# First attention of a two-block network: gate chunks as seven half products

## Chip, cores and metric

One Trainium2 chip, one core of it, one launch. The metric is device time in microseconds; lower is better. TensorE (PE) multiplies into PSUM, VectorE (DVE) and ScalarE (ACT) work on SBUF and PSUM, GpSimd (POOL) on SBUF, and SyncE (SP) issues the weight transfers.

## What is computed

The network has a first block and two layers of a second block, all in float32 on 256 tokens (512 with context) and 1024 features. The change touches the gates of the first block's mixer. Cut to what matters:

```
h = rms_norm(x, attn_pre_norm)                       # 256 x 1024
proj = h @ w_in                                      # a_qkv | b_q | b_kv | c_qkv | gates
o_a, o_b, o_c = dilated_attention(..), sliding_window_gqa(..), stick_breaking_attention(..)
g = sigmoid(gates.reshape(b, s, 3, 1024) + b_gate)   # gates: 3072 columns
merged = g[0] * (o_a @ w_br_a) + g[1] * (o_b @ w_br_b) + g[2] * (o_c @ w_br_c)
return merged @ w_out
```

The gates need h alone, so their product with 3072 columns of `w_in` can stand anywhere before `merged`.

## The kernel before

Weights come as a stream of chunks of 1024 x 256 numbers (1 MB) into a ring of four slots (`ring`). SP requests chunk c when PE has finished chunk c - 4 (`chunk_done`). Activations stand features by tokens in `H`; the 256 tokens of the first block use its columns 0 to 255.

The first attention runs in 32 **units** (`units1`): one head and one half of 128 queries each. Units 0 to 7 are branch a (three groups of keys at once), 8 to 23 branch b, 24 to 31 branch c (stick breaking, no softmax). Even units see 128 keys a group, odd ones 256. In each turn u of the loop PE does, in a written order: `scores1(u)`, the first half of a filling chunk, `turn1(u-1)` (transposes of the probabilities), the second half, `values1(u-1)`. DVE does `probs1(u-1)` (normalising, or for branch c a chain with a scan), `rows1(u)` (bias and row maximum), `turned1(u-1)` (copy of the transposed probabilities out of PSUM), then its part of the filling chunk. ACT does the exponentials, its part of the filling chunk and the copy of the values. Each engine keeps this order, so a long step on DVE holds all that stands behind it.

The filling chunks are `gates` in units 1, 4 and 6 of every eight (`GATE_AT`; twelve chunks of 256 columns) and the modulation `ada0` (24 chunks, M = 32, short). A gate chunk is two half chunks of eight matmuls of 256 tokens into PSUM bank pair 0; DVE adds the bias to one half and ACT to the other in the same unit, as soon as the whole chunk is done (`beside`, `gate_out`).

Other places of the kernel already form a chunk by **seven half products** instead of eight (`pe_fast`): four of 128 x 128 x 128 matmuls each, three with the weights as they are and four with sums of weights that POOL makes (`pool_sums`, four additions of 128 x 512 a chunk into `SUMS`, two buffers), and with differences of the activations that DVE makes once (`dve_turn`). ACT and DVE then put the four blocks together from the products (`act_fast`, `dve_fast`). The gated feed-forward of the first block (`upv`) does so with 128 tokens a product. In the first attention POOL has nothing to do.

Of the kernel before, what the change touches and what calls it, by code (L numbers as in the profile page):

```python
# [9 lines left out]
P = 128  # L10
D = 1024
KT = D // P
T1 = 256
# [3 lines left out]
SLOTS = 4  # L17
# [111 lines left out]

FAST = {"upv": 1, "down": 4, "q0": 1, "k0": 1, "v0": 1, "k1": 1, "v1": 1, "ssd_o0": 2, "out20": 1, "mlp1a0": 1, "mlp2a0": 2, "mlp1b0": 1, "mlp2b0": 2, "mlp11": 1, "mlp21": 4}  # L130
FIRST_SET = {"upv": 1, "down": 0, "q0": 1, "k0": 0, "v0": 0, "k1": 0, "v1": 0, "ssd_o0": 0, "out20": 1, "mlp1a0": 1, "mlp2a0": 0, "mlp1b0": 0, "mlp2b0": 0, "mlp11": 1, "mlp21": 0}
WIDTH = {"upv": P, "down": P, "mlp11": P, "mlp21": P}
ONE_SIDE = ("upv",)

# [34 lines left out]
def fast_plan():  # L169

    groups, chunks, used, n = {}, {}, [0, 0], 0
    for name, j in ORDER:
        if name not in FAST:
            continue
        chunks.setdefault(name, []).append(n)
        n += 1
        if j % FAST[name] == 0:
            g = groups.setdefault(name, [])  # L180
            side = (FIRST_SET[name] + len(g) * (name not in ONE_SIDE)) % 2
            g.append((sum(used), side, used[side]))
            used[side] += 1
    return groups, chunks
# [28 lines left out]
def program(nc, xT, stream, params, rows, consts, rel_bias, rev_hot, w_dt, scratch, cs_rows, x_kept, mrg_kept, out):  # L213
    ctx = ExitStack()
    with ctx:
# [255 lines left out]

        fast_free = [sem("fast_free0"), sem("fast_free1")]
        swapped = [sem("q_swapped"), sem("k_swapped")]
# [233 lines left out]
        def act_fast(act, name, keep, then_=None, beside_=None, only=None):  # L707


            share, width = FAST[name], WIDTH.get(name, T1)  # L710
            for i, (f, side, before) in enumerate(FAST_GROUPS[name]):
                if only is not None and i != only:
                    continue
                if name in ("v0", "v1"):
                    act.wait_ge(sem("v_group"), (0 if name == "v0" else 4) + i + 1)
                else:
                    act.wait_ge(chunk_done, CHUNKS[name][share * i + share - 1] + 1)
                nc.scalar.activation(keep[side], fast_bank(side, 2)[:, 0:width], ACT.Copy).then_inc(sem("fast_kept"), 1)  # L718
# [180 lines left out]
        HM1 = area(B1_GATE, 4, 4, P)  # L899
        HID1_T = area(B1_GATE + 2048, 4, 16, P)  # L900

        U_L = [area(B1_TMP + 768 * i, 768) for i in range(2)]
# [174 lines left out]
        def _(pe):  # L1077
# [62 lines left out]
            def ada_second(name, j):  # L1140
# [12 lines left out]
                mm.then_inc(sem("ada_turned"), 1)  # L1153

            def beside(items, T, t):

                if t == 0:
                    held.finish(ada_second)
                for name, j in items:
                    modulation = name.startswith("ada")  # L1160
                    if modulation and t == 0:
# [86 lines left out]
            pe.wait_ge(sem("u_out_read"), len(units1))  # L1248
            pe.wait_ge(sem("u_read_a"), len(units1) - N_AB)

            def sums_behind(tag):
# [458 lines left out]
        def _(act):  # L1710
# [38 lines left out]

            def gate_out(bank, j, it):  # L1750
                return copy(one(GATE, 2 * j + 1, 2, it), bank[:, 0:T1], ACT.Identity,
                            bias=par[:, span(PARAMS["b_gate"][0] + 2 * j + 1, 2, it)])

            bar()
# [15 lines left out]
            def beside(items, op):  # L1770
                for name, j in items:
                    if name.startswith("ada"):
                        if j % ADA_RUN == ADA_RUN - 1:
                            held.pending = (name, j)
                        continue
                    pair, before = GROUPS[name][j]
# [43 lines left out]
            pair, before = GROUPS["gates"][-1]  # L1820
            act.wait_ge(evacuated[pair], 2 * before + 2)
            for j in range(4):
# [464 lines left out]
        def _(v):  # L2287
# [64 lines left out]

            def gate_out(bank, j, it):
# [116 lines left out]
            for u in range(len(units1) + 1):  # L2470
# [4 lines left out]
                if u >= 1:  # L2475
                    turned1(u - 1)
                if u < len(units1):
                    beside(attention_fill(-1)[u], gate_out)
            for j in range(4):
# [587 lines left out]
        def _(pool):  # L3067
# [19 lines left out]
            pool.wait_ge(sem("bias_in"), 16)  # L3087
            bar()

            for j in range(4):  # L3090
# [267 lines left out]
```

## Time and profile before

| | |
|---|---|
| median of 3 runs | 2996.71 us (2996.35 to 3005.4) |
| profiled execution | 3000.34 us, its span 2998.5 us |
| mean granted PE clock | 0.994 |
| PE busy | 2923.9 us, 98% of the span |
| DVE, ACT, POOL busy | 48%, 27%, 34% |
| first attention | units begin at 128.71 us, branch products at 312.24 us |

Times in the rows count from the span's start. PE is busy nearly always, but the number counts matmuls that overlap; whether a stage is bound by PE or by the chain of waits between the engines is read from idle time in brackets in the timeline. Float32 matmuls have two records each, so "x16" is eight matmuls.

### The profile page before, as it was taken

What the parts mean: (1) busy time and instruction counts of PE and PEld (TensorE: products, weight loads), DVE (VectorE), ACT (ScalarE), POOL (GpSimd) and SP (SyncE); (2) the same over time, 40 slices, a digit from 0 to 9 for tenths busy, and PEclk for the clock granted to TensorE, in tenths of its full rate; (3) what the DMA queues carried; (4) which work ended last, traced back from release to release, by engine and by line L of the source; (5) the groups of instructions that cost most, each with busy time, mean ns of one, the idle gap of its engine ahead of it and who ended that gap; (6) DMA issues with size and microseconds to landing.
All of it is one profiled execution on the core that took longest, in us unless ns stands there. A gap on an engine that the chain in (4) does not pass through costs nothing.

```text
span 2998.5 us, 40516 instructions
## 1 busy us (share of the span) xinstructions
PE 2923.9 (98%) x16088; PEld 2388.8 (80%) x16088; DVE 1453.4 (48%) x2765; ACT 814.4 (27%) x1778; POOL 1020.8 (34%) x876
## 2 busy tenths in 40 slices
PE   8999999999999999999999999999998999999999
PEld 7776789998865548888878888888886666678998
DVE  1243268722255647777753442342237555541651
ACT  1022132201022316666610220110114355540210
POOL 0000134484310115565654244443330112110786
PEclk9999999999999999999999999999999999999999
DMA  7455434442355232222232122222330332334443
GB/s 260 142 201 219 155 127 163 161 169 99 99 185 206 87 128 100 112 105 107 90 135 84 71 85 84 87 97 85 112 113 29 128 106 99 113 107 153 155 169 113
DMA packets 68977, 377.63 MB, mean 126 GB/s; under 512 B 6378, under 2 KB 24874, under 8 KB 26304
## 3 DMA queue, kind: packets, MB, share of 16 engines
q1 hardware_dynamic: 49120, 334.60, 30.8%
q10 hardware_dynamic: 18704, 36.90, 3.7%
q0 software_dynamic: 976, 3.63, 0.3%
q8 instruction: 127, 2.08, 0.3%
q14 instruction: 50, 0.41, 0.0%
HBM read 366.50 MB, written 4.42 MB: 124 GB/s over the span
## 4 chain that ended last, share of the span: by engine, by line
PE 61%; DVE 7%; ACT 2%; PEld 1%; issue 1%; POOL 0%; PEldq 0%; POOLq 0%; ACTq 0%; DVEq 0%
PE PB L501 12%; PE PB L629 9%; PE PA L501 7%; PE PB L1480 6%; PE PS L501 6%; PE PB L381 5%; PE PB L1187 2%; PE PB L1453 2%; PE PB L425 2%; PE PA L1540 1%; PE PA L1576 1%; PE PA L1559 1%; DVE work L2871 1%; ACT work L1951 1%; PE PB L1494 1%; DVE small L2670 1%
## 5 line engine op out<-in xcount | busy, mean ns | idle before, releaser
L536 POOL TENSOR_TENSOR sums<-ring 128x512 f32<-128x512 f32 x115 | 151.6, 1318 | 603.8 <-PE PA L501 247.1
L501 PE MATMUL PB<-work,sums 128*128 128x128 f32 (+1 forms) x1360 | 230.5, 327 | 0.0
L1480 PE MATMUL PB<-H,ring 128*128 128x512 f32 (+1 forms) x576 | 228.2, 545 | 0.0
L501 PEld LDWEIGHTS PB<-work,sums 128*128 128x128 f32 x1360 | 207.0, 191 | 17.6
L501 PE MATMUL PA<-work,sums 128*128 128x128 f32 (+1 forms) x1280 | 208.9, 318 | 0.0
L734 DVE TENSOR_TENSOR work<-PA,work 128x128 f32<-128x128 f32 (+1 forms) x53 | 18.9, 357 | 379.6 <-ACT work L718 379.6
L501 PEld LDWEIGHTS PA<-work,sums 128*128 128x128 f32 x1280 | 187.4, 191 | 13.6
L3170 POOL TENSOR_TENSOR work<-work 128x256 f32<-128x256 f32 x96 | 59.8, 644 | 386.3 <-ACT work L2039 327.1
L1480 PEld LDWEIGHTS PB<-H,ring 128*128 128x128 f32 x576 | 108.4, 190 | 95.2 <-issue 90.9
L1187 PE MATMUL PB<-H,ring 128*128 128x256 f32 (+1 forms) x640 | 175.5, 429 | 0.4 <-DVE rstd L2387 0.2
L734 DVE TENSOR_TENSOR work<-PB,work 128x256 f32<-128x256 f32 (+1 forms) x34 | 13.0, 381 | 320.8 <-ACT work L718 320.8
L1187 PEld LDWEIGHTS PB<-H,ring 128*128 128x128 f32 x640 | 120.4, 193 | 46.5 <-issue 33.0
L541 POOL TENSOR_TENSOR sums<-ring,sums 128x512 f32<-128x512 f32 x115 | 151.9, 1321 | 9.0
L381 PE MATMUL PB<-work,ring 128*128 128x256 f32 (+1 forms) x544 | 153.0, 442 | 1.5 <-DVE work L2775 0.7
L539 POOL TENSOR_TENSOR sums<-sums,ring 128x512 f32<-128x512 f32 x115 | 149.7, 1302 | 0.0
L537 POOL TENSOR_TENSOR sums<-ring 128x512 f32<-128x512 f32 x115 | 148.7, 1293 | 0.0
L718 ACT ACTIVATE work<-PS 128x128 f32<-128x128 f32 (+1 forms) x53 | 17.5, 330 | 478.1 <-PE PA L501 431.1
L501 PE MATMUL PB<-work,ring 128*128 128x128 f32 (+1 forms) x840 | 143.5, 325 | 0.0
L629 PE MATMUL PB<-work 128*128 128x256 f32 x624 | 143.2, 382 | 0.0
L381 PEld LDWEIGHTS PB<-work,ring 128*128 128x128 f32 x544 | 103.0, 190 | 49.9 <-issue 39.6
L501 PEld LDWEIGHTS PB<-work,ring 128*128 128x128 f32 x840 | 127.0, 191 | 10.4
L501 PE MATMUL PS<-work,ring 128*128 128x128 f32 (+1 forms) x760 | 133.7, 319 | 0.0
(439 smaller groups left out, 5980.1 us busy)
## 6 DMA issues: line engine op xcount, KB each, us to landing
ring<-stream SPq DMA_DIRECT2D x314, 1024.0 KB, 4.8
sums<-cs_rows ACTq DMA_DIRECT2D x16, 1024.0 KB, 4.6
sums<-cs_rows ACTq DMA_DIRECT2D x16, 512.0 KB, 3.8
work<-work ACTq DMA_DIRECT2D x16, 256.0 KB, 4.5
work<-scratch POOLq DMA_DIRECT2D x1, 2560.0 KB, 13.6
mrg_kept<-work ACTq DMA_DIRECT2D x1, 2048.0 KB, 10.4
work<-mrg_kept ACTq DMA_DIRECT2D x1, 2048.0 KB, 10.6
X<-xT SPq DMA_DIRECT2D x2, 512.0 KB, 5.7
```

The source lines that it names most:

```text
L381: mm = pe.matmul(PB[:, pair, t, 0:T], ring[:, c % SLOTS, k, t * P:(t + 1) * P], rhs(k), start=(k == 0), stop=(k == KT - 1))
L425: mm = pe.matmul(PB[:, pair, t, 0:T], ring[:, c % SLOTS, k, t * P:(t + 1) * P], rhs(KT * part + k), start=(part == 0 and k == 0), stop=(pa ...
L501: mm = pe.matmul(fast_bank(side, bank)[:, col:col + width], weight(k), right(4 * part + k), start=first and opens and k == 0, stop=last an ...
L536: nc.gpsimd.tensor_tensor(su[:, 0], a21, a22, ALU.add).then_inc(sem("w_summed"), 1)
L537: nc.gpsimd.tensor_tensor(su[:, 2], a11, a21, ALU.subtract).then_inc(sem("w_summed"), 1)
L539: nc.gpsimd.tensor_tensor(su[:, 1], su[:, 0], a11, ALU.subtract).then_inc(sem("w_summed"), 1)
L541: nc.gpsimd.tensor_tensor(su[:, 3], a12, su[:, 1], ALU.subtract).then_inc(sem("w_summed"), 1)
L629: mm = pe.matmul(fast_bank(0, bank)[:, col:col + T1], weight(k), right(k), start=opens and k == 0, stop=k == 3, skip_group_check=True)
L1187: mm = pe.matmul(PB[:, pair, t, 0:T], ring[:, c % SLOTS, k, t * P:(t + 1) * P], H[:, k, 0:T], start=(k == 0), stop=(k == KT - 1))
L1453: mm = pe.matmul(PB[:, pair, t, 0:T], ring[:, c % SLOTS, k, t * P:(t + 1) * P], H[:, k, 0:T], start=(k == 0), stop=(k == KT - 1))
L1480: mm = pe.matmul(PB[:, pair, t, 0:Tc], ring[:, c % SLOTS, k, t * P:(t + 1) * P], H[:, k, 0:Tc], start=(k == 0), stop=(k == KT - 1))
L3170: gp.tensor_tensor(XD[d].rearrange("p (a b) -> p a b", a=4), XG[:, t, :].rearrange("p (a b) -> p a b", a=4), WD[:, t, heads].unsqueeze(2). ...
```

## The change

All twelve gate chunks go over to seven half products of 128 tokens. `dve_turn` makes the differences of h once, early, into the free half of `H`. POOL makes the weight sums of each chunk (`pool_sums(pool, "gates")`) from the end of the barrier before the units. PE does four products where the first half chunk stood and three where the second stood (`gate_products`). The seven results lie in bank pair 0's first half and ACT copies one of them (`act_fast`); DVE puts the blocks together in `gate_out`, seven operations, **one turn later**, behind `turned1(u-1)`; the next gate chunk and the end of the stage wait for that (`fast_free[2]`).

```diff
+            def gate_products(j, t):
+                c, n = CHUNKS["gates"][j], FAST_CHUNKS["gates"][j]
+                w, su = ring[:, c % SLOTS], SUMS[:, n % 2]
+                def product(bank, high, opens, weight, right):
+                    for k in range(4):
+                        mm = pe.matmul(gate_part(bank, high), weight(k), right(k), start=opens and k == 0, stop=k == 3,
+                                       skip_group_check=True)
+                    return mm
+                if t == 0:
+                    take_chunk(pe, c, 0, 0)
+                    if j:
+                        pe.wait_ge(fast_free[2], j)
+                    product(2, 0, True, lambda k: w[:, 2 * k, 0:P], lambda k: H[:, 2 * k, 0:P])
+                    product(0, 0, True, lambda k: w[:, 2 * k + 1, 0:P], lambda k: H[:, 2 * k + 1, 0:P])
+                    product(3, 0, False, lambda k: w[:, 2 * k + 1, P:2 * P], lambda k: h1_turned(3, k))
+                    pe.wait_ge(sem("w_summed"), 4 * n + 1)
+                    product(2, 1, False, lambda k: su[:, 0, k, :], lambda k: h1_turned(0, k))
+                    return
+                pe.wait_ge(sem("w_summed"), 4 * n + 2)
+                product(1, 1, False, lambda k: su[:, 2, k, :], lambda k: h1_turned(2, k))
+                pe.wait_ge(sem("w_summed"), 4 * n + 3)
+                product(0, 1, False, lambda k: su[:, 1, k, :], lambda k: h1_turned(1, k))
+                pe.wait_ge(sem("w_summed"), 4 * n + 4)
+                product(1, 0, False, lambda k: su[:, 3, k, :], lambda k: H[:, 2 * k + 1, P:T1]).then_inc(chunk_done, 1)
...
+                    if name == "gates":
+                        act_fast(act, name, H1_KEEP[0:1] * 3, only=j)
+                        continue
...
+            dve_turn(v, H[:, :, 0:T1], [H[:, 4 * (n % 2):4 * (n % 2) + 4, T1 + P * (n // 2):T1 + P * (n // 2) + P]
+                                        for n in range(4)], 4,
+                     lambda: v.wait_ge(sem("n1_h"), 2 * KT), sem("h1_turned"), P)
...
-            def gate_out(bank, j, it):
-                return vec.tensor_scalar(one(GATE, 2 * j, 2, it), bank[:, 0:T1],
-                                         par[:, span(PARAMS["b_gate"][0] + 2 * j, 2, it)], None, ALU.add)
+            def gate_out(j):
+                f, side, before = FAST_GROUPS["gates"][j]
+                keep, (u2, u4, u3) = H1_KEEP[0], H1_U
+                bias = [p_("b_gate", 2 * j + t) for t in range(2)]
+                v.wait_ge(sem("fast_kept"), f + 1)
+                vec.tensor_tensor(u2, gate_part(0, 1), keep, ALU.add).then_inc(sem("dve_step"), 1)
+                u2_done = next_step(dve_steps)
+                vec.scalar_tensor_tensor(GATE[:, 2 * j, 0:P], gate_part(0, 0), bias[0], keep, ALU.add, ALU.add)
...
+                vec.tensor_tensor(u4, gate_part(2, 1), u2, ALU.add).then_inc(sem("dve_step"), 1)
+                vec.tensor_tensor(u3, gate_part(1, 1), u2, ALU.add).then_inc(sem("dve_step"), 1)
+                for t in range(2):
+                    vec.scalar_tensor_tensor(GATE[:, 2 * j + t, P:T1], gate_part(1, t), bias[t], u4, ALU.add, ALU.add)
+                vec.scalar_tensor_tensor(GATE[:, 2 * j + 1, 0:P], u3, bias[1], gate_part(3, 0), ALU.add, ALU.subtract)\
+                    .then_inc(fast_free[2], 1)
...
                 if u >= 1:
                     turned1(u - 1)
+                if u and u - 1 in GATE_AT:
+                    gate_out(GATE_AT.index(u - 1))
                 if u < len(units1):
-                    beside(attention_fill(-1)[u], gate_out)
+                    beside([x for x in attention_fill(-1)[u] if x[0] != "gates"], None)
...
             bar()
+            pool_sums(pool, "gates")
```

The order of PE's instructions shows it at units 17 and 18, a gate unit of branch b and the one behind it. L1205 are scores, L1187 the gate chunk, L1218 transposes, L1227 values, L1179 an `ada0` chunk. Before:

```order
L1205 MATMUL PB<-work 128x256
L1187 MATMUL PB<-H,ring 128x256 x8
L1218 MATMUL PA<-con,work 128x128
L1187 MATMUL PB<-H,ring 128x256 x8
L1227 MATMUL PA<-work 64x128
L1205 MATMUL PS<-work 128x128
L1218 MATMUL PA<-con,work 128x128 x2
L1179 MATMUL PA<-ring,cact 32x256 x8
L1227 MATMUL PA<-work 64x128 x2
```

Now (L1250 scores, L1176 products, L1263 transposes, L1272 values, L1224 `ada0`):

```order
L1250 MATMUL PB<-work 128x256
L1176 MATMUL PB<-H,ring 128x128 x12
L1176 MATMUL PB<-H,sums 128x128 x4
L1263 MATMUL PA<-con,work 128x128
L1176 MATMUL PB<-H,sums 128x128 x12
L1272 MATMUL PA<-work 64x128
L1250 MATMUL PS<-work 128x128
L1263 MATMUL PA<-con,work 128x128 x2
L1224 MATMUL PA<-ring,cact 32x256 x8
L1272 MATMUL PA<-work 64x128 x2
```

Nothing else moved on PE: sixteen matmuls of 256 tokens became twenty-eight of 128 around the same transposes.

DVE at the same place. L2354 is the old `gate_out`, L2447 to L2450 are `probs1`, L2414 to L2420 `rows1`, L2466 is `turned1`. Before, from the end of unit 17's chunk:

```order
L2354 TENSOR_SCALAR work<-PB,par 128x256
L2447 TENSOR_TENSOR small<-small 128x1
L2449 RECIPROCAL small<-small 128x1
L2450 TENSOR_SCALAR work<-work,small 128x256
L2414 TENSOR_TENSOR work<-PS,work 128x128
L2419 TENSOR_REDUCE small<-work 128x1
L2420 TENSOR_TENSOR small<-small 128x1
L2466 COPY work<-PA 128x256
L2447 TENSOR_TENSOR small<-small 128x1
```

Now, from `probs1(17)` on (L2511 to L2514 `probs1`, L2478 to L2484 `rows1`, L2530 `turned1`, L2406 to L2418 the new `gate_out`):

```order
L2511 TENSOR_TENSOR small<-small 128x1
L2513 RECIPROCAL small<-small 128x1
L2514 TENSOR_SCALAR work<-work,small 128x256
L2478 TENSOR_TENSOR work<-PS,work 128x128
L2483 TENSOR_REDUCE small<-work 128x1
L2484 TENSOR_TENSOR small<-small 128x1
L2530 COPY work<-PA 128x256
L2406 TENSOR_TENSOR work<-PB,work 128x128
L2408 SCALAR_TENSOR_TENSOR work<-PB,par,work 128x128
L2410 TENSOR_TENSOR work<-PB,work 128x128
L2412 TENSOR_TENSOR work<-PB,work 128x128
L2416 SCALAR_TENSOR_TENSOR work<-PB,par,work 128x128 x2
```

One operation in front of `probs1(17)` went, and seven (with a last L2418) stand between `turned1(17)` and `probs1(18)`.

## Rows read from the trace of the kernel before

**Rows 1.** Waits of PE in 128:312 (us in total, times, longest)

```profile
PE PA L1218 <- DVE work L2441: 5.0, 3, 2.5
```

**Rows 2.** Timeline of PE, units 17 and 18 (start us, us, instructions, [idle before])

```profile
233.25 0.44 PE L1218 MATMUL PA<-con,work 128*128 128x128 f32 x2 [0.46 <-DVE work L2450]
...
235.82 0.33 PE L1218 MATMUL PA<-con,work 128*128 128x128 f32 x1
```

**Rows 3.** Timeline of PE in the feed-forward: plain chunk, seven half products, plain chunk

```profile
409.16 7.07 PE L1303 MATMUL PB<-H,ring 128*128 128x256 f32 x32
416.07 1.05 PE L501 MATMUL PS<-H,ring 128*128 128x128 f32 x8
...
422.32 7.07 PE L1303 MATMUL PB<-H,ring 128*128 128x256 f32 x32
```

**Rows 4.** Timeline of DVE: first evacuation of a projection chunk

```profile
28.66 0.42 DVE L2342 TENSOR_SCALAR work<-PB 128x256 f32<-128x256 f32 x1 [1.91 <-PE PB L381]
```

**Rows 5.** Timeline of DVE in the feed-forward (convolution steps, block assembly)

```profile
404.16 1.78 DVE L2547 SCALAR_TENSOR_TENSOR work<-PB,par,work 128x255 f32<-128x255 f32 x4 [3.34 <-ACT work L1857]
409.67 0.29 DVE L734 TENSOR_TENSOR work<-PA,work 128x128 f32<-128x128 f32 x1 [3.73 <-ACT work L718]
409.88 0.28 DVE L736 TENSOR_TENSOR work<-PA,work 128x128 f32<-128x128 f32 x1
```

**Rows 6.** Timeline of DVE, units 17 and 18

```profile
233.10 0.28 DVE L2414 TENSOR_TENSOR work<-PS,work 128x128 f32<-128x128 f32 x1
...
233.82 0.42 DVE L2466 COPY work<-PA 128x256 f32<-128x256 f32 x1
234.71 0.16 DVE L2447 TENSOR_TENSOR small<-small 128x1 f32<-128x1 f32 x1 [0.46 <-ACT work L1801]
...
235.10 0.29 DVE L2450 TENSOR_SCALAR work<-work,small 128x128 f32<-128x128 f32 x1
```

**Rows 7.** Timeline of DVE: `probs1(15)`, `turned1(20)`, `probs1(23)`

```profile
221.32 0.16 DVE L2447 TENSOR_TENSOR small<-small 128x1 f32<-128x1 f32 x1 [0.27 <-ACT work L1801]
...
247.68 0.29 DVE L2466 COPY work<-PA 128x128 f32<-128x128 f32 x1
...
260.43 0.16 DVE L2447 TENSOR_TENSOR small<-small 128x1 f32<-128x1 f32 x1 [0.71 <-ACT work L1801]
```

**Rows 8.** Timeline of PE: end of gate 14, start of gate 22, `turn1(25)`

```profile
217.01 1.07 PE L1179 MATMUL PA<-ring,cact 128*32 128x256 f32 x16
...
248.80 3.72 PE L1187 MATMUL PB<-H,ring 128*128 128x256 f32 x16
...
273.65 0.44 PE L1218 MATMUL PA<-con,work 128*128 128x128 f32 x2 [1.78 <-DVE work L2441]
```

**Rows 9.** Timeline of DVE in the feed-forward: `dve_turn` without and with POOL at work

```profile
399.79 0.29 DVE L758 TENSOR_TENSOR work<-work 128x128 f32<-128x128 f32 x1
...
414.86 1.24 DVE L758 TENSOR_TENSOR work<-work 128x128 f32<-128x128 f32 x1
```

**Rows 10.** Timeline of POOL at that time

```profile
414.21 1.73 POOL L536 TENSOR_TENSOR sums<-ring 128x512 f32<-128x512 f32 x1 [8.05 <-DMA ring<-stream]
415.91 1.31 POOL L537 TENSOR_TENSOR sums<-ring 128x512 f32<-128x512 f32 x1
```

**Rows 11.** One line's instructions, L2600: duration ns min/median/max

```profile
L2600 DVE TENSOR_SCALAR work<-work,par x8: 346/982/1356, 621.3 to 696.6; 128x256 f32<-128x256 f32 x8
```

**Rows 12.** One line's instructions, L734: duration ns min/median/max

```profile
L734 DVE TENSOR_TENSOR work<-PB,work x34: 290/424/425, 619.8 to 2961.6; 128x256 f32<-128x256 f32 x23, 128x128 f32<-128x128 f32 x11
```

**Rows 13.** Landing of weight chunks (SP's issues, 128:312)

```profile
DMA to landing us min/median/max: 4.6/4.8/7.8
```

**Rows 14.** Timeline of DVE: first and last operation of `probs1(25)`, branch c

```profile
271.53 0.42 DVE L2435 TENSOR_TENSOR work<-work 128x256 f32<-128x256 f32 x1
...
273.17 0.42 DVE L2441 TENSOR_TENSOR work<-work 128x256 f32<-128x256 f32 x1
```

**Rows 15.** Busy time by stretch: us, PE, PEld, DVE, ACT, POOL, PEclk, DMA, GB/s

```profile
275.20:285.40 10.20, 10.20 (x38) 6.28 (x38) 2.75 (x9) 1.65 (x6) 0.00 (x0) 0.50 0.58 212
```

More of the change, by code:

```diff
@@ L127, in chunk_order @@
     return order
[L130 to L133, printed above, removed]
+FAST = {"gates": 1, "upv": 1, "down": 4, "q0": 1, "k0": 1, "v0": 1, "k1": 1, "v1": 1, "ssd_o0": 2, "out20": 1, "mlp1a0": 1, "mlp2a0": 2, "mlp1b0": 1, "mlp2b0": 2, "mlp11": 1, "mlp21": 4}
+FIRST_SET = {"gates": 2, "upv": 1, "down": 0, "q0": 1, "k0": 0, "v0": 0, "k1": 0, "v1": 0, "ssd_o0": 0, "out20": 1, "mlp1a0": 1, "mlp2a0": 0, "mlp1b0": 0, "mlp2b0": 0, "mlp11": 1, "mlp21": 0}
+WIDTH = {"gates": P, "upv": P, "down": P, "mlp11": P, "mlp21": P}
+ONE_SIDE = ("upv", "gates")
 SCAN_FAST = ("ssd0", "z0", "gs0")
@@ L169, in fast_plan @@
 def fast_plan():
-    groups, chunks, used, n = {}, {}, [0, 0], 0
+    groups, chunks, used, n = {}, {}, [0, 0, 0], 0
     for name, j in ORDER:
@@ L180, in fast_plan @@
             g = groups.setdefault(name, [])
-            side = (FIRST_SET[name] + len(g) * (name not in ONE_SIDE)) % 2
+            side = FIRST_SET[name] if name in ONE_SIDE else (FIRST_SET[name] + len(g)) % 2
             g.append((sum(used), side, used[side]))
@@ L470, in fast_bank, with gate_part @@
                 else (PA[0], PA[1], PS[:, 0], PS[:, 1])[i]
-        fast_free = [sem("fast_free0"), sem("fast_free1")]
+        def gate_part(bank, high):
+            at = 2 * P * (bank % 2) + P * high
+            return PB[:, 0, bank // 2, at:at + P]
+        fast_free = [sem("fast_free0"), sem("fast_free1"), sem("fast_free2")]
         swapped = [sem("q_swapped"), sem("k_swapped")]
@@ L717, in act_fast @@
                     act.wait_ge(chunk_done, CHUNKS[name][share * i + share - 1] + 1)
-                nc.scalar.activation(keep[side], fast_bank(side, 2)[:, 0:width], ACT.Copy).then_inc(sem("fast_kept"), 1)
+                kept = gate_part(2, 0) if name == "gates" else fast_bank(side, 2)[:, 0:width]
+                nc.scalar.activation(keep[side], kept, ACT.Copy).then_inc(sem("fast_kept"), 1)
                 if beside_:
@@ L900, in program, with h1_turned @@
         HID1_T = area(B1_GATE + 2048, 4, 16, P)
+        H1_KEEP = [area(25608 + P * i, P) for i in range(2)]
+        H1_U = [area(25864 + P * i, P) for i in range(3)]
+        def h1_turned(n, q):
+            return H[:, 4 * (n % 2) + q, T1 + P * (n // 2):T1 + P * (n // 2) + P]
         U_L = [area(B1_TMP + 768 * i, 768) for i in range(2)]
@@ L1249, in _ @@
             pe.wait_ge(sem("u_read_a"), len(units1) - N_AB)
+            pe.wait_ge(fast_free[2], len(GATE_AT))
             def sums_behind(tag):
@@ L1748, in _ @@
             evac(act, 1, "c_v", lambda bank, j, it: copy(V1[:, 1, 896:1152], bank[:, 0:CHUNK], ACT.Copy))
-            def gate_out(bank, j, it):
-                return copy(one(GATE, 2 * j + 1, 2, it), bank[:, 0:T1], ACT.Identity,
-                            bias=par[:, span(PARAMS["b_gate"][0] + 2 * j + 1, 2, it)])
             bar()
@@ L1774, in beside @@
                             held.pending = (name, j)
+                        continue
+                    if name == "gates":
+                        act_fast(act, name, H1_KEEP[0:1] * 3, only=j)
                         continue
@@ L1814, in _ @@
                     softmax1(u)
-                    beside(attention_fill(-1)[u], gate_out)
+                    beside(attention_fill(-1)[u], None)
                 if u >= 1:
@@ L1818, in _ @@
             held.finish(ada_second)
-            pair, before = GROUPS["gates"][-1]
-            act.wait_ge(evacuated[pair], 2 * before + 2)
+            act.wait_ge(fast_free[2], len(GATE_AT))
             for j in range(4):
@@ L2476, in _ @@
                     turned1(u - 1)
+                if u and u - 1 in GATE_AT:
+                    gate_out(GATE_AT.index(u - 1))
                 if u < len(units1):
-                    beside(attention_fill(-1)[u], gate_out)
+                    beside([x for x in attention_fill(-1)[u] if x[0] != "gates"], None)
             for j in range(4):
```

7 lines of the change are left out of this document (6 added, 1 removed).

## Prediction

> **What bounds the kernel now.** I read the page first (PE busy 98%, so time is won only where PE's own work shrinks and PE really is what is waited for), then PE's timeline and its waits from 128 to 312 us, then DVE's, ACT's and SP's timelines of the same units, and last the feed-forward stage, which already runs the form that the gates are to get. In the first attention PE mostly has work, but not everywhere: it sits idle ahead of transposes until DVE has made the probabilities. The reader is to see three such waits behind branch c's last step, 5.0 us in all, 2.5 the longest [rows 1]; 1.78 us of it stand at unit 25 [rows 8]. They follow gate units: the old `gate_out` waits for the whole chunk and holds `probs1` of the same unit, so the next transposes are late. At unit 18 the same thing costs 0.46 us [rows 2]. So this stage hangs between PE and DVE, and a change that takes work from PE and gives work to DVE is to be costed on both.
>
> **The change part by part.**
>
> *PE's work.* In the feed-forward a plain chunk of 32 records starts at 409.16 and the seven half products behind it at 416.07: 6.91 us. These last until 422.32: 6.25 us [rows 3]. So a gate chunk gets 0.66 us shorter, not an eighth of its multiplications' 6.91 (0.86). The split around the transposes stays as it is. Twelve chunks: **-7.9 us**.
>
> *Waits that go.* `gate_out` no longer stands in front of `probs1` of its own unit. The waits at units 9 and 17, 0.46 us each ([rows 2], of which unit 9 is a repeat), 25 with 1.78 [rows 8] and 28 with the remaining 5.0 - 2.5 - 1.78 = 0.7 [rows 1] lose their cause: **-3.4 us**. The one of 2.5 is at unit 31, behind the last `ada0` chunk, and stays.
>
> *Waits that come: DVE.* The new `gate_out` has three two-tensor additions, which the block assembly of the feed-forward issues 0.21 us apart, and four operations with a bias. A convolution step of this kind on 255 columns takes 1.78 / 4 = 0.44 us [rows 5]; 127 columns fewer at the 0.13 us by which 128 columns more lengthen such operations (0.29 to 0.42 in [rows 6]) leave 0.31. Sum 0.6 + 1.2 = 1.8 us, against 0.4 of the old one. It stands behind `turned1(u-1)`, and queued behind it are `probs1(u)`, for which PE's next transposes wait, and `rows1` of the next unit.
> - Units 2, 5: branch a's fill is long enough, nothing. Units 13 and 21: `probs1` is hidden behind the next gate chunk's first half, but that chunk needs the bank that `gate_out` is still reading. `turned1(20)` starts at 247.68 and gate 22 at 248.80 [rows 7, 8]: 247.68 + 0.2 + 1.8 = 249.7, so +0.9. The same at 14, and about 0.4 at 30: +2.2.
> - Units 10, 18, 26, directly behind a gate of the pattern's first place. From the end of its scores, unit 18 needs on DVE its rows (233.10 to 233.82, 0.72), the copy (0.35), now 1.8, and its probabilities (234.71 to 235.39, 0.68): 3.6 us [rows 6]. PE, which then starts `turn1(17)` at once, is at `turn1(18)` after 235.82 - 233.25 = 2.57 us [rows 2]. Wait about 1.1; 1.4 in branch c, whose chain is longer: +3.6.
> - Units 7, 15, 23, behind a gate unit that has an `ada0` chunk too. DVE's slack ahead of the probabilities is only 0.27 us at 15 and 0.71 at 23 (7 is like 23) [rows 7]; 1.8 less that is 1.5 + 1.1 + 1.1: +3.7.
>
> Sum: **+9.5 us**.
>
> *Waits that come: POOL.* Up to now POOL is idle in this stage. A subtraction on 128 columns with both inputs in SBUF takes 0.29 us while POOL rests and 1.24 while POOL adds weights: it starts at 414.86 and ends at 416.10, just behind the end of POOL's operation at 415.94 [rows 9, 10]. A scalar product from SBUF goes from 0.35 to as much as 1.36 us [rows 11]. Operations with an input in PSUM don't suffer: all of the assembly's additions stay within 0.43 us, whatever POOL does in those stages [rows 12], so `gate_out` itself is safe. In the attention the blocked kinds are the tiny sum and the scaling in `probs1` (branch b), and all four operations of branch c's chain. The Trainium skill ("SBUF — State Buffer", section "SBUF: two separate sides") says that a VectorE operation in a two-port mode or with two SBUF inputs and a GpSimd operation that reads SBUF exclude each other for a whole instruction. The rows agree; no row here shows the scan of branch c beside POOL, which by that rule is held as well, and without which the sum would be about 1 us less.
>
> When does POOL run? A gate's weights are requested when the chunk four ahead is done and land 4.8 us later [rows 13]; then four additions of 1.3 us [rows 10]. For gate 17 that chunk is gate 14, done at 217.01 [rows 8]: POOL runs from 221.8 to 227, right on `probs1(15)`, which [rows 7] put at 221.3 and the new `gate_out` at 222.8. Two held operations there: +1.3. Gate 25 hangs on gate 22 in the same way and hits `probs1(23)`: +1.5. Gates 9 and 17 lose about 0.9 together at units 7 and 17. For gate 28 the transfers queue, and POOL meets `probs1(25)`: four held operations of 1.3 us in place of the 2.06 us from 271.53 to 273.59 [rows 14] would keep the wait there at up to 2.9; it is a race with the landing, so I take half, 1.5. Sum **+5.2 us**, between 0 (all misses) and 7. The weights themselves come in time: gate 17's last sum is ready 4.8 + 5.2 = 10 us behind gate 14's end, and its last product, about 2 us ahead of the 233.25 of [rows 2], is due after 14.
>
> *The differences of h.* Four operations ahead of the first evacuation on DVE, each at most the 1.24 us of [rows 9] though POOL rests, together at most 5 us. DVE idles 1.91 us there [rows 4]; what runs over delays one evacuation whose bank PE wants a chunk later, 6.9 us on [rows 3]. Nothing; without that cover 3 us.
>
> *The clock.* The wait of 1.78 us at unit 25 was followed by a stretch of 10.2 us at a granted 0.50, the lower level, 1.2 GHz, on a PE that was busy throughout [rows 15]: 5.1 us. Now 15 and 23 get waits of about 3 us, and 25 keeps one. I count half of one more such stretch: **+2.5 us**, between 0 and 10.2 (two whole ones).
>
> Sum: -7.9 - 3.4 + 9.5 + 5.2 + 2.5 = **+5.9 us**. Against the profiled execution's 3000.34 us (span 2998.5 and 1.84 around it) that is 3006.2; that execution is 3.6 us above the median of the runs, as long as most of such a clock stretch. From the median of 2996.71: **3002.6 us**.
>
> **Rivals.** *DVE's work is hidden after all and POOL misses.* For it: DVE is busy less than half the time. Against it: rows 6 and 7 show the slack place by place. With half the new waits and no held operation: -7.9 - 3.4 + 4.8 = -6.5, 2990 us; with none of them -11.3, 2985.4. This is the case on the fast side; it wins by over 0.3% only if less than 2.3 us of new waits come.
>
> *The clock falls at each long wait.* Same sum with two whole stretches more: -7.9 - 3.4 + 9.5 + 5.2 + 10.2 = +13.6, 3010.3 us. It decides from the point where waits at 15 and 23 reach the 1.78 us that the one at unit 25 had. For it: the sum gives them 2.6 to 2.8. Against it: a stretch need not be 10 us long.
>
> *The change moves nothing,* because the stage is bound by DVE and ACT throughout: 2996.7. Against it: most gate halves follow each other on PE without idle time.
>
> **How the numbers follow.** 0.3% is 9.0 us, about what a measurement of this kernel can tell from no change. My sum, with part of one more clock stretch: 0.50, 2997 to 3006. Two whole stretches, or longer waits: 0.25, 3005 to 3012. Nothing moved: 0.08. Waits mostly hidden: 0.17, 2985 to 2995. Faster than 2987.7 is half of the last, 0.08. Slower than 3005.7 is the second and a little of the first, 0.28. Same: 0.64. The range leaves out a tenth on each side: from 2989, where half the DVE waits are hidden, to 3010, two stretches.
>
> **What the profile would show.** Gate halves of about 3.6 and 2.7 us. POOL in the stage with 12 x 5.2 = 62 us. No wait ahead of `turn1(9)` and `turn1(17)`; new ones of about 1 us ahead of `turn1` at 10 and 18, of 2.5 to 3.5 at 15 and 23, and 0.9 ahead of gates 14 and 22. `probs1(15)`'s two SBUF operations stretched to 1 us or more. A lower granted clock behind unit 15 or 23. The prediction is wrong if POOL's additions fall into gate halves in which DVE rests, or if `gate_out` takes much less than 1.8 us.

## The result, and the profile after

The changed kernel takes 3004.76 us (median of 20 runs, 2996.85 to 3015.39), the kernel before 2997.22 us in the same sessions (20 runs, 2995.49 to 3007.18). The ratio is 1.002, 95% interval 1.0011 to 1.0028: 3 to 8 us slower, under the 9 us that count as a change here (ratio and interval come from all runs, not from the two medians). Forecast were 3002.6 us and "same".

The page of the changed kernel, span and busy times of the engines:

```profile
span 2998.7 us, 41227 instructions
...
PE 2917.1 (97%) x16376; PEld 2394.4 (80%) x16376; DVE 1484.5 (50%) x2841; ACT 812.0 (27%) x1778; POOL 1081.0 (36%) x924
```

POOL has 60 us more than before (1020.8) and PE 7 us less. The gain on PE is there, and the time is not. PE's waits in 128:315, grouped (us in total, times, longest), say where it went; their counterpart is [rows 1]:

```profile
PE PA L1263 <- DVE work L2514: 6.8, 5, 2.1
PE PA L1263 <- DVE work L2505: 4.5, 3, 2.5
...
PE PB L1176 <- DVE work L2418: 2.1, 3, 0.9
PE PA L1164 <- DVE rstd L2432: 1.1, 1, 1.1
```

L2514 is `probs1`'s scaling, for which the transposes (L1263) wait; L2505 is the last operation of branch c's chain, for which they wait there; L2418 is `gate_out`'s last operation, for which the next gate chunk waits; L2432 is DVE's copy of a modulation run. The timeline of PE gives the places (start us, duration us, [idle before <- releaser]):

```profile
179.81 0.66 PE L1263 MATMUL PA<-con,work 128*128 128x128 f32 x4 [1.53 <-DVE work L2514]
...
196.19 0.33 PE L1263 MATMUL PA<-con,work 128*128 128x128 f32 x1 [0.80 <-DVE work L2514]
...
209.26 2.92 PE L1176 MATMUL PB<-H,ring 128*128 128x128 f32 x24 [0.87 <-DVE work L2418]
...
221.51 0.62 PE L1164 MATMUL PA<-con,rstd 128*128 128x24 f32 x4 [1.11 <-DVE rstd L2432]
...
223.67 0.69 PE L1263 MATMUL PA<-con,work 128*128 128x128 f32 x2 [1.54 <-DVE work L2514]
...
241.13 0.33 PE L1263 MATMUL PA<-con,work 128*128 128x128 f32 x1 [0.80 <-DVE work L2514]
...
267.47 0.44 PE L1263 MATMUL PA<-con,work 128*128 128x128 f32 x2 [2.12 <-DVE work L2514]
...
278.19 0.44 PE L1263 MATMUL PA<-con,work 128*128 128x128 f32 x2 [0.74 <-DVE work L2505]
...
282.08 0.33 PE L1263 MATMUL PA<-con,work 128*128 128x128 f32 x1 [1.25 <-DVE work L2505]
```

In order (gate 14 is the gate chunk of unit 14): `turn1(7)`, `turn1(10)`, gate 14, unit 15 (twice: ahead of a modulation run's turn and of `turn1(15)`), `turn1(18)`, `turn1(23)`, `turn1(25)`, `turn1(26)`; gate 22 waits 0.87 us like gate 14, gate 30 0.32 us. The waits of 0.46 us at units 9 and 17 [rows 2] are gone, and 25 has 0.74 in place of 1.78 us [rows 8]. DVE's timeline at units 17 and 18 shows both causes:

```profile
235.24 1.25 DVE L2514 TENSOR_SCALAR work<-work,small 128x256 f32<-128x256 f32 x1
...
238.44 0.43 DVE L2530 COPY work<-PA 128x256 f32<-128x256 f32 x1
238.78 0.28 DVE L2406 TENSOR_TENSOR work<-PB,work 128x128 f32<-128x128 f32 x1
...
240.40 0.15 DVE L2511 TENSOR_TENSOR small<-small 128x1 f32<-128x1 f32 x1
...
240.79 0.29 DVE L2514 TENSOR_SCALAR work<-work,small 128x128 f32<-128x128 f32 x1
```

From 238.78 to 240.40 DVE puts the gate's blocks together, and `probs1(18)` stands behind it; `turn1(18)` waits until 241.13. The first row is the other cause: a scaling that takes 0.35 us elsewhere takes 1.25 us, and it ends at 236.49, just behind this operation of POOL's, which ends at 236.33:

```profile
235.06 1.27 POOL L547 TENSOR_TENSOR sums<-ring,sums 128x512 f32<-128x512 f32 x1
```

The third is the clock. Busy time by stretch (us, PE, PEld, DVE, ACT, POOL, PEclk, DMA share, GB/s), behind units 7 and 15 and behind unit 31:

```profile
181.20:184.60 3.40, 3.40 (x24) 2.43 (x13) 1.15 (x5) 0.48 (x3) 0.00 (x0) 0.50 0.44 94
...
222.20:232.40 10.20, 8.73 (x43) 6.15 (x44) 4.75 (x13) 1.98 (x9) 4.95 (x5) 0.50 0.56 231
...
307.50:317.70 10.20, 8.58 (x24) 6.57 (x25) 0.81 (x2) 6.15 (x7) 0.00 (x0) 0.50 0.34 121
```

These stretches run at the lower level, 1.2 GHz. That behind unit 25 [rows 15] is gone, and two new ones follow the new waits at units 7 and 15. The wait of 2.12 us at unit 23 is followed by none.

### The profile page after: what moved, and what is told of

The parts are those of the page before. It is cut to its first block, busy times and chain, and to the rows that moved or that the text cites. A ratio compares the mean times of both kernels' runs of the same rounds, so it can differ in the third digit from the quotient of the medians.

```text
span 2998.7 us, 41227 instructions
## 1 busy us (share of the span) xinstructions
PE 2917.1 (97%) x16376; PEld 2394.4 (80%) x16376; DVE 1484.5 (50%) x2841; ACT 812.0 (27%) x1778; POOL 1081.0 (36%) x924
## 4 chain that ended last, share of the span: by engine, by line
PE 61%; DVE 7%; ACT 1%; PEld 1%; issue 1%; POOL 0%; PEldq 0%; POOLq 0%; ACTq 0%; DVEq 0%
PE PB L507 12%; PE PB L635 9%; PE PA L507 7%; PE PB L1526 6%; PE PS L507 6%; PE PB L381 5%; PE PB L1232 2%; PE PB L1499 2%; PE PB L425 2%; PE PA L1586 1%; PE PA L1622 1%; PE PA L1605 1%; DVE work L2937 1%; ACT work L1995 1%; PE PB L1540 1%; DVE small L2736 1%
## 5 line engine op out<-in xcount | busy, mean ns | idle before, releaser
L542 POOL TENSOR_TENSOR sums<-ring 128x512 f32<-128x512 f32 x127 | 166.5, 1311 | 797.1 <-DMA ring<-stream 256.9
L1526 PEld LDWEIGHTS PB<-H,ring 128*128 128x128 f32 x576 | 108.4, 190 | 95.2 <-issue 90.9
L547 POOL TENSOR_TENSOR sums<-ring,sums 128x512 f32<-128x512 f32 x127 | 167.3, 1317 | 10.0
L545 POOL TENSOR_TENSOR sums<-sums,ring 128x512 f32<-128x512 f32 x127 | 165.5, 1303 | 0.0
L543 POOL TENSOR_TENSOR sums<-ring 128x512 f32<-128x512 f32 x127 | 164.0, 1291 | 0.0
L725 ACT ACTIVATE work<-PB 128x128 f32<-128x128 f32 (+1 forms) x46 | 15.2, 330 | 450.6 <-PE PB L507 346.6
L507 PEld LDWEIGHTS PB<-work,ring 128*128 128x128 f32 x840 | 127.0, 191 | 10.4
L635 PEld LDWEIGHTS PB<-work 128*128 128x128 f32 x624 | 116.6, 190 | 17.6 <-issue 1.7
```

Source lines behind the costliest of these rows:

```text
L507: mm = pe.matmul(fast_bank(side, bank)[:, col:col + width], weight(k), right(4 * part + k), start=first and opens and k == 0, stop=last an ...
L542: nc.gpsimd.tensor_tensor(su[:, 0], a21, a22, ALU.add).then_inc(sem("w_summed"), 1)
L543: nc.gpsimd.tensor_tensor(su[:, 2], a11, a21, ALU.subtract).then_inc(sem("w_summed"), 1)
L545: nc.gpsimd.tensor_tensor(su[:, 1], su[:, 0], a11, ALU.subtract).then_inc(sem("w_summed"), 1)
L547: nc.gpsimd.tensor_tensor(su[:, 3], a12, su[:, 1], ALU.subtract).then_inc(sem("w_summed"), 1)
L635: mm = pe.matmul(fast_bank(0, bank)[:, col:col + T1], weight(k), right(k), start=opens and k == 0, stop=k == 3, skip_group_check=True)
```

## The experiments

"Stage" is the time from unit 0's scores to the first branch product in the profiled execution (before: 128.71 to 312.24 us). "Rest" is the span from there to its end, in which all fourteen kernels are alike. "Low" is the part of the stage at a granted clock of 0.50. Ratios are to the kernel before, with 95% intervals; a, b, c and so on are the places in the text below.

| kernel | median us | ratio | stage | low | rest |
|---|---|---|---|---|---|
| before | 2997.22 | 1 | 183.5 | 13.2 | 2686.3 |
| changed | 3004.76 | 1.002 (1.0011 to 1.0028) | 184.3 | 18.1 | 2686.8 |
| a. POOL without its sums | 2997.0 | 0.999 (0.9978 to 1.0002) | 176.9 | 7.0 | 2692.0 |
| b. one assembly operation | 2993.7 | 0.9977 (0.9961 to 0.9993) | 178.5 | 18.7 | 2687.0 |
| c. neither | 2984.51 | 0.9953 (0.9934 to 0.9971) | 167.7 | 4.1 | 2686.4 |
| d. assembly in its own unit | 3019.9 | 1.0065 (1.0043 to 1.0088) | 207.5 | 53.6 | 2686.8 |
| e. early assembly | 2998.69 | 0.9992 (0.9976 to 1.0009) | 174.4 | 6.7 | 2692.3 |
| f. half of it early | 2994.91 | 0.999 (0.998 to 0.9999) | 177.9 | 7.9 | 2686.6 |
| g. sums in pieces | 2995.51 | 0.9996 (0.9986 to 1.0005) | 180.3 | 10.4 | 2692.2 |
| h. e and g together | 2985.83 | 0.9957 (0.994 to 0.9974) | 169.0 | 4.9 | 2687.1 |
| i. h, PE kept busy | 2988.53 | 0.9959 (0.9943 to 0.9975) | 169.3 | 0 | 2682.8 |
| j. before, PE kept busy | 2998.0 | 0.9988 (0.9975 to 1.0) | 180.5 | 0 | 2693.2 |
| k. changed, PE kept busy | 3003.16 | 1.0008 (0.9995 to 1.002) | 190.1 | 10.2 | 2686.3 |
| l. h, last scaling first | 2979.75 | 0.9937 (0.9918 to 0.9956) | 165.9 | 0 | 2682.8 |

**a, b, c: the two costs, each away and both.** In a, `pool_sums` adds one column of 128 for the gates from the third chunk on:

```diff
+                m = 1 if name == "gates" and n >= 2 else P
+                su = su[:, :, :, 0:m]
```

> Left out: from the third gate chunk on POOL adds only one column of each weight sum instead of 128 (half the sums' values are stale), so POOL holds nothing of DVE's for long; PE and DVE do all their work. Theory (the saving on PE is eaten by three things: the 1.8 us block assembly on DVE, POOL holding DVE's scalings, and the clock): the scalings (L2514) take .3 us each time, the waits of PE in front of turn1(7), turn1(15) and turn1(23) fall by .4 to 1.5 us each, those at units 10, 18, 26 and 14, 22, 30 stay at .3 to 1.2 us; the stage (scores of unit 0 to the branch products, 184.3 us in the changed kernel's profile) is 4 to 6 us shorter, the time near 2999.5 us. Rival (the assembly alone eats it): the stage is no more than 1 us shorter. Rival (the clock alone): the waits stay, only the low-clock stretches differ.

The stage is 7.4 us shorter than the changed kernel's, and more than half of that is the clock's (11.1 us less at the lower level; the price stands under j). From the timeline of PE, units 7, 10, 15 and 23:

```profile
179.75 0.66 PE L1265 MATMUL PA<-con,work 128*128 128x128 f32 x4 [1.07 <-DVE work L2516]
...
194.68 0.33 PE L1265 MATMUL PA<-con,work 128*128 128x128 f32 x1 [0.80 <-DVE work L2516]
...
220.00 0.62 PE L1166 MATMUL PA<-con,rstd 128*128 128x24 f32 x4 [1.11 <-DVE rstd L2434]
...
259.80 0.44 PE L1265 MATMUL PA<-con,work 128*128 128x128 f32 x2 [1.44 <-DVE work L2516]
```

7 and 23 lose 0.5 and 0.7 us, 15 its second wait of 1.54; 25 has none. 10 and 18 keep their 0.80 to the digit, gates 14 and 22 have 0.86 for 0.87. So POOL's part and DVE's part are told apart by place. In b, `gate_out` keeps its last operation alone:

```diff
-                vec.tensor_tensor(u2, gate_part(0, 1), keep, ALU.add).then_inc(sem("dve_step"), 1)
...
+                vec.scalar_tensor_tensor(GATE[:, 2 * j + 1, 0:P], gate_part(1, 0), bias[1], keep, ALU.add, ALU.add)\
```

> Left out: six of the seven DVE operations that assemble a gate chunk (the rest of the gate tiles is a constant, written once by POOL at the first chunk); PE's half products and POOL's sums are all there. Theory: the new waits of PE behind units 10, 18, 26 (.80, .80, 1.25 us) and at gates 14, 22, 30 (.87, .87, .32) are gone, those at 7, 15, 23 fall by some .5 us each; the stage is 7 to 9 us shorter than the changed kernel's, the time near 2996. Rival (POOL's hold alone): those six waits shrink by no more than .3 us each, the time stays above 3002. Rival (the clock alone): the waits stay.

The waits at 10 and at gates 14, 22 and 30 are gone. Two of the six stayed, against the expectation, and both are longer than in the changed kernel (timeline of PE, `turn1(18)` and `turn1(26)`):

```profile
232.51 0.33 PE L1265 MATMUL PA<-con,work 128*128 128x128 f32 x1 [1.02 <-DVE work L2506]
...
274.01 0.35 PE L1265 MATMUL PA<-con,work 128*128 128x128 f32 x1 [1.81 <-DVE work L2497]
```

With DVE ahead by the missing work, `probs1(18)` and `probs1(26)` now fall on POOL's sums: the one's scaling takes 1.18 us, and of the other's four operations two take over a microsecond, the scan among them, which takes 0.42 us elsewhere (h, unit 30). From b's timeline of DVE:

```profile
271.06 1.36 DVE L2493 TENSOR_TENSOR_SCAN work<-work 128x128 f32<-128x128 f32 x1
...
272.46 1.17 DVE L2496 TENSOR_TENSOR work<-work,con 128x128 f32<-128x128 f32 x1
```

In c both costs are away.

> Left out: both, six of the seven assembly operations and all but a column of the weight sums, so that what stays is PE's part of the change. Theory: it shows the saving on PE by itself, 7.9 us of work and 3.4 us of waits off the stage of the kernel before (183.5 us), and no new wait above .3 us: a stage of 172 to 174 us, a time of 2985 to 2989. Rival (the saving was never there: weights or the chain of the softmax bound the stage): a stage above 180 us, waits on landings or on ACT in the place of those on DVE.

It is 15.8 us shorter in the stage than the kernel before, more than expected, and holds no new wait (timeline of PE: `turn1(23)` has 0.60 as before the change, and the branch products begin):

```profile
254.27 0.44 PE L1267 MATMUL PA<-con,work 128*128 128x128 f32 x2 [0.60 <-DVE work L2508]
...
296.30 5.49 PE L1320 MATMUL PB<-work,ring 128*128 128x256 f32 x12 [0.66 <-ACT work L1857]
```

The rival that the saving isn't there falls. From c, the assembly alone brings 9.2 us back (a), POOL alone 10.8 (b), both 16.6 (changed), all of the saving. The single ones make 20.0 together, since the clock falls differently in each: by the price of j (0.44 us for each us at the lower level), 1.3, 6.4 and 6.2 us of these are clock, estimated, and without it the assembly costs 7.9, POOL 4.4 and both 10.4.

**d: the assembly in its own unit,** behind `turned1(u-1)` and before `probs1(u)`.

```diff
-                if u and u - 1 in GATE_AT:
-                    gate_out(GATE_AT.index(u - 1))
                 if u < len(units1):
+                    if u in GATE_AT:
+                        gate_out(GATE_AT.index(u))
```

> Nothing left out: the assembly of a gate's blocks stands in its own unit again (behind that unit's rows, before the scaling of its probabilities), where the kernel before had its eviction. Theory: DVE now waits for the chunk's last product and holds the scaling of the same unit behind 1.8 us of assembly, so turn1 of the gates' own units waits 1 to 2 us at twelve places, and the waits behind units 10, 18, 26 and at 14, 22, 30 go: 5 to 15 us slower than the changed kernel, 3010 to 3020. Rival (the place of the assembly doesn't matter, only its work): within 2 us of the changed kernel.

15 us slower than the changed kernel. The stage is 23.2 us longer, about 15.6 of it by 35.5 us more of lower clock (estimated by the price of j), the rest by waits. These stand ahead of the transposes of the gates' own units, 0.5 to 5.4 us at ten of the twelve, 9 and 25 the longest, and those at 10, 18, 26 and at gates 14, 22, 30 are gone (timeline of PE):

```profile
195.05 0.69 PE L1263 MATMUL PA<-con,work 128*128 128x128 f32 x2 [2.50 <-DVE work L2514]
...
293.97 0.69 PE L1263 MATMUL PA<-con,work 128*128 128x128 f32 x2 [5.40 <-DVE work L2505]
```

So "one unit later" was needed; the place decides more than the work does.

**e, f: a better place.** The products of the first part are p20, p00, p30, p01, those of the second p21, p11, p10, each part in a bank of its own, so that `gate_first` can read the first while PE fills the second. The seven operations stay seven; in e they stand between `probs1(u)` and `rows1(u+1)`, in f the last four behind `turned1(u)`.

```diff
                 if u >= 1:
                     probs1(u - 1)
+                    if u - 1 in GATE_AT:
+                        gate_first(GATE_AT.index(u - 1))
+                        gate_out(GATE_AT.index(u - 1))
```

> Nothing left out. The four products of the gates' first part now fill one PSUM bank, the three of the second the other; the kept product is copied, and three of the seven assembly operations made, as soon as the first bank is done; all seven stand between the scaling of the gates' unit and the rows of the next one, where DVE idles about 1.75 us, in the place of behind the copy of the turned blocks. Theory: the assembly is hidden as far as POOL leaves DVE alone: the waits behind units 10, 18, 26 (.80, .80, 1.25 us) and at gates 14, 22, 30 fall to .3 us or less, those at 7, 15, 23 stay between those of the run with one operation and those of the changed kernel; a stage near 179 us (the run with one operation had 178.5), a time of 2992 to 2998. Rival (the work of the assembly counts, wherever it stands): the waits move to the rows and scalings of the next unit, the stage stays above 183 us.

> Nothing left out. As the run before in this call, but the four late assembly operations stand where the changed kernel has all seven, behind the copy of the turned blocks. Theory: 1.15 us are left there in the place of 1.73, so the waits behind units 10, 18 and 26 fall by about .6 us each, those at gates 14, 22, 30 too: a stage between the early version's and the changed kernel's, near 181 us. Rival (the place doesn't matter): the same as the early version within 1 us.

In e the waits at gates 14, 22, 30, at 15 and 25 went, that at 7 is 0.23 us as before the change, and the stage fell by 9.9 us. But 10, 18 and 26 kept theirs (0.91, 1.01, 2.12), against the expectation (timeline of PE, `turn1(18)`):

```profile
234.39 0.33 PE L1264 MATMUL PA<-con,work 128*128 128x128 f32 x1 [1.01 <-DVE work L2520]
```

Here the scaling takes 1.17 us beside POOL's last sum: b's miss again. f has a stage between e and the changed kernel, as expected, though of the three waits behind units 10, 18 and 26 only the first got shorter (0.28, 1.02 and 2.34 us). Neither median shows much; e's profile has a rest 5.5 us longer (last section).

**g, h: shorter operations on POOL.** Each sum of 512 columns as four of 128:

```diff
+                    for k in range(0, 4, step):
+                        ins = nc.gpsimd.tensor_tensor(to[:, k:k + step], x[:, k:k + step], y[:, k:k + step], op)
+                    ins.then_inc(sem("w_summed"), 1)
```

> Nothing left out. The changed kernel, with each of POOL's 512 column sums of the gates made in four instructions of 128 columns. Theory (POOL holds DVE's scaling until its running instruction ends): the scalings that took 1.06 to 1.25 us take .3 to .7 us, the waits in front of turn1(7), turn1(15) and turn1(23) fall by .4 to .8 us each; a stage 2 to 5 us shorter than 184.3, a time of 2998 to 3002. Rival (POOL slows DVE as long as any sum is under way): the scalings take as long as before and the stage stays within 1 us, or is longer by what the 12 more instructions of each chunk take.

> Nothing left out. Early assembly and the sums in four pieces together. Theory: the two costs fall together and what is left is near PE's own saving: a stage of 170 to 176 us (the run with neither cost had 167.7), a time of 2986 to 2992, some .2 to .35% under the kernel before. Rival (the costs don't add up, since either alone fills DVE's slack): no better than the early version alone by more than 1 us.

In g the scaling of unit 17, 1.25 us in the changed kernel, takes 0.71 us (timeline of DVE); POOL needs 1.7 us a sum for 1.27 (timeline of POOL, a sum in four pieces). The scaling ends at 232.83, while the pieces go on: DVE is held by the instruction that runs, not by POOL's being at work.

```profile
232.12 0.71 DVE L2521 TENSOR_SCALAR work<-work,small 128x256 f32<-128x256 f32 x1
```

```profile
231.82 1.74 POOL L546 TENSOR_TENSOR sums<-sums,ring 128x128 f32<-128x128 f32 x4
```

Alone it gains 4.0 us of stage, most of it clock (7.7 us less at the lower level, 3.4 by the price of j): `turn1(15)` waits 0.32 us for 1.54, but 7 only 0.14 us less than in the changed kernel, and 10 and 26 longer (1.09 and 1.79). With e's order nearly everything is back: h is within 1.3 us of c, and does all the work. `turn1(10)` and `turn1(18)` wait at most 0.11 us there, `turn1(26)` 0.32 us. DVE's timeline of h at unit 20 shows the early three from 239.53, the late four from 241.10, and the next unit's rows at 242.23:

```profile
239.53 0.28 DVE L2413 TENSOR_TENSOR work<-PB,work 128x128 f32<-128x128 f32 x1
...
241.10 0.29 DVE L2426 TENSOR_TENSOR work<-PB,work 128x128 f32<-128x128 f32 x1 [0.83 <-PE PB L1186]
...
242.23 0.42 DVE L2491 TENSOR_TENSOR work<-PB,work 128x256 f32<-128x256 f32 x1
```

**i, j, k: the clock.** PE multiplies for nobody ahead of long waits:

```diff
+            def keep_busy(n):
+                for i in range(n):
+                    pe.matmul(PS[:, 1, 0:P], ident, ident, start=True, stop=True)
```

> Nothing left out; 18 products of 128 columns whose result nobody reads are added ahead of turn1(31), where PE waits 2.52 us for the last scaling. Base: early assembly with the sums in four pieces. Theory (the clock falls behind a long wait and costs more than the wait): the wait is filled, the low-clock stretch that followed it for 10.24 us in the base's profile is gone or starts after the branch products, and the time is 2 to 5 us under the base's 2985.8: 2981 to 2984. Rival (the clock falls for what the stage as a whole did): the stretch stays and the time is within 1 us of the base.

> Nothing left out. The kernel before the change with such products, 13 ahead of turn1(25) and 18 ahead of turn1(31), in waits of 1.78 and 2.52 us. Theory: both low-clock stretches of its stage (10.24 us behind unit 25, 6.8 us behind unit 31) are gone, which are about 4 and 2 us of lost time: the stage is 4 to 7 us under 183.5, the time 2990 to 2993. So that much of what the kernel with neither cost saved was the clock's and not the half products'. Rival: the stage stays within 1 us of 183.5, and the whole of 15.8 us is the half products'.

> Nothing left out. The changed kernel with such products in its long waits: 11 ahead of turn1(7), 8 ahead of unit 15's modulation turn and 11 ahead of turn1(15), 15 ahead of turn1(23), 5 and 18 ahead of turn1(25) and turn1(31). The waits for DVE stay as long. Theory: the low-clock stretches behind units 7, 15 and 31 are gone (3.4, 10.2 and 10.2 us in the changed kernel's profile, some 1.7, 4 and 4 us of lost time); the stage is 6 to 10 us under 184.3 and the time 2994 to 2999, so that the new waits alone cost some 5 us less than they seemed to. Rival (the clock has no part): within 1 us of the changed kernel's 3004.8.

The products were sized wrong: each is two records, so 18 of them take this long (timeline of PE in i) in a wait of 2.52 us:

```profile
290.96 4.29 PE L1290 MATMUL PS<-con 128*128 128x128 f32 x36
```

In j this costs 1.2 us ahead of `turn1(25)` (3.01 us between its first product and the transposes, for a wait of 1.78) and 1.6 ahead of `turn1(31)` (4.12 for 2.52). The stretch that ran at 0.50 before [rows 15] runs at 1.00 (busy time by stretch):

```profile
272.50:285.40 12.90, 12.90 (x98) 10.01 (x98) 5.89 (x18) 2.10 (x8) 0.00 (x0) 1.00 0.64 246
```

The stage is 3.0 us shorter, which with 2.8 of overrun makes 5.8 us that 13.2 us of low clock cost the kernel before: 0.44 us for each, an estimate from this one pair of profiles. The median stayed (2998.0), against the expectation. In i the stretch of h at 0.50 behind unit 31 (10.2 us) is gone too; the profile shows 5 us less of span. The median doesn't: four of its runs take 2982 to 2986 us at a mean granted clock of 0.997 to 0.998, and four 2991 to 2992 at 0.994. The latter hold more low clock; where it lies was not profiled. k tells little: filled too long as well, it lost the stretches behind units 7 and 15 and got others behind 18 and 26:

```profile
240.90:247.70 6.80, 6.80 (x36) 5.39 (x29) 1.91 (x9) 1.74 (x7) 4.58 (x4) 0.50 0.58 214
```

So a filler moves the clock, but on the changed kernel it didn't pay.

**l: the remaining wait.** In h, DVE reached unit 31's scaling chain late because the copy of the last modulation run stood ahead of it.

```diff
                     probs1(u - 1)
+                    if u == len(units1):
+                        beside(attention_fill(-1)[u - 1], None)
...
-                if u < len(units1):
+                if u < len(units1) - 1:
                     beside([x for x in attention_fill(-1)[u] if x[0] != "gates"], None)
```

> Nothing left out. Early assembly with the sums in four pieces, and in the last turn DVE scales unit 31 before it copies the last modulation run, for whose product it waited from 290.57 to 292.13 us. Theory: the wait of 2.52 us in front of turn1(31) falls to .5 to 1.0 us, and with it perhaps the low-clock stretch behind it: 2980 to 2984 us. Rival (the wait moves to the modulation's turn, which now comes later): within 1 us of 2985.8.

The wait of 2.52 us is 0.56 (timeline of PE), no stretch of the stage has a lower clock, and the median is 17.8 us under the kernel before, the lowest of all. Against h the stage is 3.1 us shorter, about 2.2 of it clock by the price of j, and the intervals of the two overlap.

```profile
291.72 0.44 PE L1271 MATMUL PA<-con,work 128*128 128x128 f32 x2 [0.56 <-DVE work L2518]
...
294.54 2.86 PE L1324 MATMUL PB<-work,ring 128*128 128x256 f32 x12 [0.66 <-ACT work L1861]
```

## Why the prediction was right, step by step

| step | forecast us | measured us |
|---|---|---|
| PE's work | -7.9 | -8.4: c is 15.8 shorter than before; 3.4 are waits, 9.1 x 0.44 = 4.0 clock |
| waits that go | -3.4 | -3.4 in c; -2.6 in the changed kernel, 25 keeping 0.74 |
| waits by DVE | +9.5 | +7.7: all waits of a less those that c keeps at the same places |
| waits by POOL | +5.2 | +4.3 (b less c, the same way) |
| the two together | +14.7 | +11.1 (changed less c) |
| `dve_turn` of h | 0 | 0 seen: units begin at 127.60, before at 128.71 us |
| clock | +2.5 | +2.2 in the profiled pair: 18.1 - 13.2 = 4.9 us more of low clock, x 0.44; about +4.9 over all runs, see below |

The mechanism was right: PE's saving exists, and DVE's assembly, POOL's hold and the clock eat it. By the profiled pair the measured terms make -8.4 - 3.4 + 11.1 + 2.2 = +1.5, and the stages differ by +0.8. The medians differ by 7.5. Two terms were mis-sized: the waits, 14.7 for 11.1, and the clock, 2.5 for about 4.9 over the runs. The errors partly cancel, so that 3002.6 lies so near 3004.76 is in part luck. The waits by place: 10 and 18 have 0.80 (1.1 forecast, though its own rows make 0.72 + 0.35 + 1.8 + 0.68 - 2.57 = 1.0), 26 1.25 (1.4), gates 14, 22, 30 0.87, 0.87, 0.32 (0.9, 0.9, 0.4), 15 has 2.65 (2.8), 25 has 0.74 (1.5, taken as half of a race). 23 has 1.5 more than before (2.6 forecast), since POOL held one operation there and not two; 7 has 1.3 more and 17 nothing (2.0 forecast for both), because the long scaling of 17 ended at 236.49, ahead of the transposes' turn.

Why do the medians differ by more than the profiled pair? Each run has its mean granted clock on record, and at the same clock the two kernels take about the same time (median us, number of runs; the kernel before has 69 runs with a clock, from the sessions of the experiments):

| mean granted clock | before | changed |
|---|---|---|
| 0.992 | 3006.5 (16) | 3006.7 (6) |
| 0.994 | 3001.7 (10) | 3000.8 (4) |
| 0.995 | 2997.5 (14) | 2999.6 (3) |
| 0.996 | 2996.9 (21) | 2996.9 (1) |

But the changed kernel's runs have a lower clock, 0.9929 in the mean for 0.9947. The lower level being half the speed, that is 2 x 0.0018 x 3000 = 11 us more of it in a run, by 0.44 some 4.9 us (an estimate), and the means of the runs, 3004.8 and 2999.9 us, differ by 4.9 (the kernel before has 2999.1 in the 20 runs beside the changed kernel's). With it the measured terms make -8.4 - 3.4 + 11.1 + 4.9 = +4.2. The medians differ by more because 43 of the 69 runs before lie at 2995 to 2999 us and the others at 3000 to 3007, so that the median sits in the lower group. So the runs add clock to the profiled pair, and nothing else that is seen. Where its stretches lie in the longer runs, no profile shows.

What the prediction named as proof came: gate halves of 3.7 and 2.8 us, POOL with 61.8 us in the stage, `probs1(15)` stretched. `gate_out` takes 1.7 us (238.78 to 240.49) for the 1.8 of the sum. Only the wait at 23, 2.12 us, stayed under the 2.5 to 3.5 named. Of the rivals, "hidden after all" fell; without the two costs the time is where that rival put it (2985.4 us forecast, 2984.51 measured), but 4.0 us of c's gain are clock, which that rival didn't count. "The clock at each long wait" came in part: behind 7 and 15, not behind 23.

The Trainium skill ("SBUF — State Buffer", section "SBUF: two separate sides") says that VectorE, in a two-port mode or with two SBUF inputs, and GpSimd contend for a shared pair of ports as for a lock: whichever starts first has it for the whole instruction, and the other is blocked. The traces agree: the scaling of 1.25 us ends 0.16 us behind POOL's addition (236.49 and 236.33), and in g, with shorter instructions on POOL, the hold is shorter (0.71 us). The scan of branch c, for which the prediction had no row, is held too (b: 1.36 us).

## What to carry to other kernels

A saving on the bounding engine that is paid for on its neighbours is lost where the neighbour's new work stands in front of what the bounding engine waits for: look for the stretch in which the neighbour idles (here between `probs1` and the next `rows1`) and put it there. Here the results were also reordered and split over two banks, so that the first half could be read early; what that is worth by itself was not tested. Work on POOL beside a latency chain on DVE is to be cut into short instructions. Leave out each suspected cost, and then both: c showed in one profile that the stage could be 15.8 us shorter, 4.0 of it by the clock. And put the runs side by side at the same mean granted clock: that told here what the medians hid.

## What the runs showed of the hardware

The lower clock comes in stretches of 3.4, 6.8, 10.2, 13.7 (d) and 20.5 us, and where it comes differs from variant to variant. One sits far from the change, near 1000 us, behind waits of the second attention that are the same in both of the next kernels (0.66, 0.57 and 1.20 us): in the kernel before 3.3 us of it at 0.50, in j 20.3 us (busy time by stretch of before, then of j):

```profile
1009.10:1012.40 3.30, 2.84 (x14) 2.58 (x14) 1.64 (x5) 0.56 (x2) 0.00 (x0) 0.50 0.02 5
```

```profile
1007.00:1027.30 20.30, 19.44 (x80) 17.30 (x79) 3.46 (x9) 8.85 (x9) 3.06 (x3) 0.50 0.00 1
```

a, e, g and j have the long one, and their rest is 2692 to 2693 us; without it the others have 2683 to 2687. So a kernel's time holds some 5 us that the work around its edit doesn't explain, and the stage in the profile told the variants apart better. And DVE is held even in an operation of one column (128x1, L2511 in the changed kernel: 0.15 us at 240.40, but 0.54 us at 234.46 while POOL was adding).
